# Extra matmuls into an unread bank at each RMS norm between the dense stages of a two-block hybrid model

## The reference

```python
def rms_norm(x, g):
    xf = x.astype(F32)
    y = xf * lax.rsqrt(jnp.mean(xf * xf, axis=-1, keepdims=True) + NORM_EPS)
    return (y * g.astype(F32)).astype(x.dtype)

# first block, each of 2 layers
u = rms_norm(h, norm_mix_g[layer]); p = u @ w_in[layer]      # then the three mixers
h = h + merged @ w_o[layer]
u = rms_norm(h, norm_ffn_g[layer]); h = h + conv_glu(u, ...)
# then rms_norm(h, norm_final_g); second block, each of 2 layers
x = x + 0.5 * swiglu(rmsnorm(x, ffn1_norm[l]), ...)
x = x + hybrid_mixer(rmsnorm(x, mix_norm[l]), ...)
x = x + 0.5 * swiglu(rmsnorm(x, ffn2_norm[l]), ...)
# then rmsnorm(x, final_norm)
```

## Time and the profile before

| | |
|---|---|
| median of 3 timed runs | 3278.16 us (3278.11 to 3280.18) |
| the profiled execution | 3272.9 us, span 3271.1 us |
| mean granted TensorE clock | 0.918 |
| TensorE busy (matmuls) | 2856.0 us, 87% of the span |
| VectorE, ScalarE, GpSimd busy | 1945.2, 1362.7, 152.0 us |

### The profile page before, as it was taken

How to read it: one execution, slowest core, us unless ns; L and a number is a source line. 1 busy time by engine, 2 the same in 40 slices (tenths; PEclk the granted TensorE clock), 3 DMA queues, 4 the chain that set the end, 5 groups by cost and what they waited for, 6 DMA issues and landing times. The chain is left out here.

```text
span 3271.1 us, 53748 instructions
## 1 busy us (share of the span) xinstructions
PE 2856.0 (87%) x23052; PEld 2442.1 (75%) x23052; DVE 1945.2 (59%) x2620; ACT 1362.7 (42%) x1873; POOL 152.0 (5%) x116
## 2 busy tenths in 40 slices
PE   7888678889898678889998998879999988988899
PEld 6787557778787557778887785668888877756788
DVE  5754766875754766875647444566566564446564
ACT  5413344545413334555544223355454532335453
POOL 0030000000030000000000220000000003100000
PEclk9898888999898888998999898989999989889899
DMA  5211124454211114454543111144655421113353
GB/s 211 91 40 52 65 67 141 164 191 168 91 40 52 65 65 142 158 199 150 204 157 118 47 40 55 62 155 169 222 170 205 145 97 39 65 39 113 134 206 130
DMA packets 54669, 386.19 MB, mean 118 GB/s; under 512 B 6688, under 2 KB 7328, under 8 KB 8352
## 3 DMA queue, kind: packets, MB, share of 16 engines
q1 hardware_dynamic: 54432, 382.76, 33.8%
HBM read 381.69 MB, written 1.05 MB: 117 GB/s over the span
## 5 line engine op out<-in xcount | busy, mean ns | idle before, releaser
L320 PE MATMUL banks<-normed_high,weights_high 128*128 128x256 f16 (+1 forms) x4096 | 1147.8, 280 | 86.3 <-DVE weights_low L306 55.4
L321 PE MATMUL banks<-normed_low,weights_high 128*128 128x256 f16 (+1 forms) x4096 | 1146.5, 280 | 0.0
L322 PE MATMUL banks<-normed_high,weights_low 128*128 128x256 f16 (+1 forms) x4096 | 1145.2, 280 | 0.0
L306 DVE SCALAR_TENSOR_TENSOR weights_low<-weight_ring,weights_high 128x2048 f16<-128x2048 f32 x334 | 761.2, 2281 | 411.2 <-ACT weights_high L300 395.4
L300 ACT ACTIVATE weights_high<-weight_ring 128x2048 f16<-128x2048 f32 x306 | 580.2, 1898 | 291.9 <-PE banks L322 272.3
L320 PE MATMUL banks<-projected,weights_high 128*128 128x256 f16 x1696 | 473.1, 279 | 79.0 <-DVE projected L331 71.9
L320 PEld LDWEIGHTS banks<-normed_high,weights_high 128*128 128x128 f16 (+1 forms) x4096 | 411.3, 100 | 169.5 <-issue 90.4
L321 PE MATMUL banks<-projected,weights_high 128*128 128x256 f16 x1696 | 473.4, 279 | 0.0
L322 PE MATMUL banks<-projected,weights_low 128*128 128x256 f16 x1696 | 473.0, 279 | 0.0
L322 PEld LDWEIGHTS banks<-normed_high,weights_low 128*128 128x128 f16 (+1 forms) x4096 | 410.7, 100 | 58.9
L321 PEld LDWEIGHTS banks<-normed_low,weights_high 128*128 128x128 f16 (+1 forms) x4096 | 410.1, 100 | 57.6 <-issue 1.3
(11 more groups left out here) (391 smaller groups left out, 3260.7 us busy)
## 6 DMA issues: line engine op xcount, KB each, us to landing
weight_ring<-w SPq DMA_DIRECT2D x356, 1024.0 KB, 4.9
small_weights<-small SPq DMA_DIRECT2D x2, 1280.0 KB, 8.6
constants<-const SPq DMA_DIRECT2D x1, 1601.0 KB, 10.1
weight_ring<-w SPq DMA_DIRECT2D x2, 640.0 KB, 3.8
residual<-xt SPq DMA_DIRECT2D x1, 1024.0 KB, 5.1
small_weights<-small SPq DMA_DIRECT2D x2, 512.0 KB, 10.4
out<-residual SPq DMA_DIRECT2D x4, 256.0 KB, 2.8
parameters<-par SPq DMA_DIRECT2D x2, 115.5 KB, 9.4
```

The lines of the kernel that those rows point to most:

```text
L306: nc.vector.scalar_tensor_tensor(out=self.part(self.mem.w_low, g), in0=self.part(self.mem.ring, g), scalar=W_SCALE, in1=self.part(self.mem ...
L320: pe.matmul(out, w_high, high, start=start, stop=False, skip_group_check=skip)
L321: pe.matmul(out, w_high, low, start=False, stop=False, skip_group_check=skip)
L322: return pe.matmul(out, w_low, high, start=False, stop=stop, skip_group_check=skip)
```

## The change

A helper multiplies the constant `ident` (the f32 identity, read as f16, so 256 columns of two-byte numbers) by itself into one bank, `count` times, 128x128 weights and 256 columns each. `Norm` gets the number of such a bank as a third entry of `spare`. It is called three times in each norm: 8 times ahead of the last pair of tiles of the sums and ahead of the wait for its squares, 4 times behind the sums, 12 times behind the spread. No engine reads what it writes, and it waits for nothing.

```diff
+def keep_clock(pe, mem, bank, count):
+
+    still = mem.c("ident").bitcast(F16)
+    for _ in range(count):
+        pe.matmul(mem.ps[:, bank, 0:T], still[:, 0:P], still, start=True, stop=True)
...
-    def __init__(self, mem, cut, sig, gain, ready, sums, spread):
+    def __init__(self, mem, cut, sig, gain, ready, sums, spread, idle):
...
+        self.idle_bank = idle
...
     def sum(self, pe):
         for k in range(KT):
+            if k == KT - 2:
+                keep_clock(pe, self.mem, self.idle_bank, 8)
             if k % 2 == 0:
                 pe.wait_ge(self.sig("squares"), k // 2 + 1)
...
         mm.then_inc(self.sig("square_sums"), 1)
+        keep_clock(pe, self.mem, self.idle_bank, 4)
 
     def spread(self, pe):
         pe.wait_ge(self.sig("inverse"), 1)
...
         mm.then_inc(self.sig("spread"), 1)
+        keep_clock(pe, self.mem, self.idle_bank, 12)
...
-    project, low = project_stage(nc, mem, p_sig, stream, in_groups(0), 0, "mix1_0", loaded_h, (4, 6),
+    project, low = project_stage(nc, mem, p_sig, stream, in_groups(0), 0, "mix1_0", loaded_h, (4, 6, 1),
...
-        LOW_SPARE, HIGH_SPARE = (2, 2), (4, 4)
+        LOW_SPARE, HIGH_SPARE = (2, 2, 1), (4, 4, 6)
...
-        ffn2, project, low = ffn_and_project2(1, g_sig, p_sig, after_residual(f_sig), (2, 2), delta,
+        ffn2, project, low = ffn_and_project2(1, g_sig, p_sig, after_residual(f_sig), LOW_SPARE, delta,
```

## The result

| | before | after |
|---|---|---|
| median of 5 timed runs | 3280.18 us (3278.11 to 3281.11) | 3263.29 us (3260.52 to 3266.12) |
| ratio | | 0.9949, 95% interval 0.9934 to 0.9963 |
| profiled execution | 3272.9 us, span 3271.1 | 3266.12 us, span 3264.3 |
| mean granted clock | 0.918 | 0.922 |

The change makes the kernel 16.9 us faster, 0.51%.

What follows compares the result with a forecast made beforehand. Bound: TensorE, at half clock around the norms. Gains of 12.05 - 0 - 1.3 - 1.3 = 9.4 us, taken from 3278.16, give 3269 us; 8 in 10 range 3253 to 3280, the forecast's own 3260 to 3277.

Steps and rivals of the forecast that it cites:

- TensorE bounds the dense stages: Feed-forward stages behind norms: time gained on TensorE reaches the end whole; if convolution stages swallowed it, a quarter less gain.
- The added matmul is a dense one: Each of 288 added matmuls costs what a dense 128x256 one does: 0.109 us at full clock, 0.213 at half.
- The share-out: Eight norms between dense stages: three hold the clock (gain 2.9 us each), four regain it early (1.0), one late (loss 0.65).
- An early return of 6.8 us: At such a norm the clock falls as before but returns earlier; root 1.15 us late, first tile 1.0 us earlier.
- The other four norms: First norm 0; final norm of block 1 with the norm behind it (the pair) loss 1.3 us; last norm loss 1.3.
- The long stretches: Four stretches of some 500 us (projection, mixers, merge): each can give or take up to some 3 us, sign unknown.
- The granted clock is below full in every slice of the page: Reading of the profile page before the change: TensorE's clock is never full in any slice; no size given.
- All held: Rival: the clock stays up through every norm after the first; gain 27 us, 3251 us, chance 0.13.
- The no-help rival: Added matmuls bring the clock back no earlier at any norm; 11.5 us slower, 3290 us, chance 0.13.
- The cancelling rival: Few norms held; early returns paid back by first norm, pair and last: gain 0.4 us, 3278 us, chance 0.12.
- Theory M: From the experiments: long stretches run in step with the clock's change moments, so a small shift is swallowed or grows.

Runs made afterwards that it cites:

- shift8: Kernel before the change, with eight added matmuls ahead of the last sums of the very first norm and nowhere else; 3280.53 us against 3278.76, ratio 0.9999.

## Why the prediction was right, and where it was not

The forecast was a gain of 9.4 us and a time of 3269 us; measured were 16.9 us and 3263.3, inside the range and inside the forecast's own. Of the 7.5 us between them, 3.7 are at the norms (13.1 where 9.4 were forecast) and 3.8, by difference, outside them.

- *TensorE bounds the dense stages, and a gain at a norm reaches the end, in the convolution stages too.* Shown, by the equal lengths of the dense stages.
- *The added matmul is a dense one.* Shown for its cost, 421 ns at half clock, 0.213 us to the next; and twelve of it bring the clock back early, which the same number with two columns does not.
- *The share-out, three held, four early, one late, for 12.05 us.* This is the step that failed, and that its sum came close is luck. Measured are none held, none late and all eight early: 13.37 us. I had one length for an early return, 6.8 us. There were two, and the shorter one, 3.41 us, is worth 2.25 to 2.55 us, nearly the 2.9 that I had priced for a norm in which the clock is held. So a kind that I did not have stood in for one that did not occur.
- *An early return of 6.8 us gains 1.0.* Measured 1.2. The eight begin 2.6 us after the first sum, as I had it, but the root is 0.75 late and not 1.15. The last eight sums start 0.62 later than before (at 3.59 us instead of 2.97) where I had 0.75, and from there to the root it is 1.74 us instead of 1.61, where I had counted 0.4 more: before the change, too, most of these sums run at half clock.
- *The other four norms, -2.6.* Measured -0.26: the first 0.44 instead of 0, the pair 0.20 instead of -1.3, the last -0.90 instead of -1.3. In the pair the clock was up for 3.4 us between two low stretches; I had counted it low until the dense work.
- *The long stretches can give or take some 3 us each.* That they move is shown, the size was too small: the same stretch takes 485.4 or 495.7 us. In the timed runs of this change at most 3.8 of the 16.9 us are theirs, by difference; with the twelve alone it is nearly half of the 36 us (36 less 19.3 at the norms).
- *The granted clock is below full in every slice of the page.* Misread: a 9 there can be full clock. The earlier trace rows has 1.00 from 2218.41 to 2388.00 us, more than two slices long. Nothing in the sum hangs on it.

All held is refuted by every window at a norm, and with it what the Trainium skill's page "TensorE: Matmul & The Clock Gate", section "Why this matters for your kernels", would give if taken by gaps alone: after the change TensorE has no gap above 0.2 us in the norms shown, and the clock falls there all the same. The no-help rival is refuted by the 6.83 and 3.41. What it needed, added matmuls that do not bring the clock back, exists, with two columns. The cancelling rival was right that none is held; but it had three norms late, where none was, and a loss of 2.6 us at the other four, where it was 0.26.

What I did not see is that my own working for the early return called the eight a cost and named nothing that they buy. Without them and the four the kernel is 19 us faster than the change, 6.2 of it at the norms; without the eight alone it is 16.5 us faster, 7.4 of it at the norms.

It stays open why a stretch settles at one of its lengths, and whether it would with other inputs. No experiment traced one fall of the clock inside a mixer to its cause. That a longer stretch goes with a lower clock is shown by TensorE's busy time at equal counts, not which of the two causes the other; that a shift was swallowed is shown by `shift8` and by the eight alone, once each. Theory M is thus not proven. Open is also which of the added parts moves the long stretches: their total was 2014.5 us with all three, 1996.3 without the eight and 1998.5 with the eight alone.

## What to carry to other kernels

Work that is there only to bring the clock up belongs directly ahead of the dense work that is to profit, in a wait that it fills and no further. Over the norms of this kernel six matmuls in that wait won 0.4 us, ten 16.8, twelve 19.3 and eighteen 11.6; eight in front of an instruction on the path cost 12.4. They moved 256 columns each; with two columns they won nothing. And a kernel whose clock rises and falls often has to be timed several times and read stage by stage: here 2.4 us at one place were gone 510 us later, and a stretch of unchanged code differed by 10 us between kernels.

## What the runs showed of the hardware

- Matmuls with two columns each and their f32 weight loads do not keep the clock at 2.4 GHz (the first 24 of a norm keep TensorE busy for 2.73 of 2.73 us, and in the kernel before the clock falls 3.0 to 4.2 us after the first of them), nor does it return during 6.98 us of them. 24 more f16 ones with two columns change nothing; the same 24 with 256 columns shorten the low stretch from 10.24 us to 6.83 or 3.41.
- In all twelve kernels the low stretches at the plain norms last 3.41, 6.83 or 10.24 us, once 13.65; in the double norm up to 23.9.
- A chain of some 3140 matmuls with many waits between (the third and fourth long stretch) has lengths from 485.3 to 498.0 us, with the same work on the other engines and a mean clock of 0.92 to 0.88, and 2.4 us added ahead of the first long stretch, of some 3323 matmuls, were gone at its end.
